# Two units' scores per visit to the 64-row products, masks added on VectorE, up-projections in groups of four

## The chip, the core and the metric

The kernel runs on one core of one Trainium2 chip, in one launch, in float32. Weights and activations of the large products are split into a high and a low part of a reduced format that the kernel calls fp32r; three products of the parts stand for one float32 product. The metric is the device time of one execution in microseconds; the kernel before takes 871.8 us (median of three runs, 871.6 to 871.97).

## The reference

The input x (256 tokens, 1024 wide) passes two blocks. The first: differential attention and stick-breaking attention side by side, cross attention on 256 memory tokens, and an MLP with squared ReLU. The second block is where most of the change lies: attention over compressed, selected and window keys (12 heads, called nsa below), and attention with dilations (12 heads in three groups of four, called dil), then gates, an output product and another MLP. In NumPy terms, cut to what matters:

```python
# first block, differential attention: two softmaxes per head, causal
p = softmax(where(causal, q k^T * scale, -inf)); w = p[0] - lam * p[1]; o = w v
# second block, dilated attention, g = 3 groups of 4 heads (window, dilation)
s = where((d >= 0) & (d % dil == 0) & (d <= win), q k^T * scale, -1e30)
o_g = softmax(s) v;  lse_g = log(sum(exp(s)));  y = sum_g softmax_over_g(lse)_g * o_g
# second block, nsa: for selected and window keys (at 256 tokens both are causal)
o_b = softmax(where(causal, q k^T * scale, -1e30)) v_b;   y += gate_b * o_b    # b = 1, 2
# MLP
h += square(relu(norm(h) @ w_up)) @ w_down          # w_up 1024 x 4096
```

## The kernel before, in words

Weights come in strips of 512 columns (or 512 rows) by SP's DMA queue into three buffers `raw`. ScalarE (ACT) copies each half strip to its high part (`hi`, L738), GpSimd (POOL) subtracts to the low part (L695), TensorE (PE) multiplies (`strip`, whose products are L1922 in three modes, and L1928 and L1929 in the mode `up`). The order of every engine's instructions is written out by hand; semaphores join them.

The mode `up` computes 128 output columns of an up-projection in one PSUM bank: for each of the 8 blocks of 128 input rows, `both` issues one product of 512 columns (high weights by x high and x low side by side) and one of 256 columns (low weights by x high). There are 16 such strips, with 32 pairs each.

Attention is cut into units (`units`). A unit has 512 score columns in two PSUM banks, one bank for heads in rows 0 to 63 of the array, one for heads in rows 64 to 127 (head width 64, so two score products run side by side in the halves of the array). Units 0 to 5 are the differential attention, 6 to 9 the cross attention, and from `U_A` on come 27 units of the second block: 9 dil (3 for the first 128 tokens with four heads each, 6 for the others with two heads and 256 keys), 6 nsa for the first 128 tokens (two heads, two branches), and 12 nsa for the others (two heads, one branch, 256 keys). `unit_loop` runs over the units with a lag, on each engine:

- PE, turn i: masks of unit i by an identity product of bfloat16 into both banks (L2079), the score products (L2086; each float32 product is two passes in the profile), then the `hook` (a share of a strip of the next projection, so that PE has work), then the transposes of the probabilities of unit i-1 (L2098), then the products with the values of unit i-2 (L2112) into bank 7.
- DVE (VectorE), turn i: row maximum of unit i (one TENSOR_REDUCE of 512 columns, L1358), the copy of the transposed probabilities of unit i-1 to SBUF (L1368), then `post` of unit i-2. `post_nsa` is a reciprocal (L1801), a product with the gates (L1803), a product of the values by these factors (L1805, after which PE may overwrite bank 7) and one addition to `xn` per branch (L1812). `post_dil` is a copy (L1817). For the differential units there is also `combine` (L1380 to L1388), on which the transposes wait.
- ACT: exponentials with a row sum (L787), after the maximum of the same unit.

The log-sum-exp over the dilations is one Ln and one Exp on ACT and some small operations on DVE (L1836 to L1849), after which POOL mixes the three groups (L675 to L681).

At the end of the second loop, turn `NU`, PE transposes two blocks of `xn` into banks 0 and 1 (`fill_block`, L2024), ACT and DVE split them (`fill_hi`, `fill_lo_block`, L1170), and the next strip (`IN2 + 13`), which writes banks 0 to 3, waits for these splits. DVE does the first of them (`fill_lo_block(0)`) in `post_nsa` of the last unit but one.

The line that decides the scores' banks before the change:

```python
half = bank(4 - (4 if n >= U_A else 2) * (n % 2), 2).rearrange("p (r x) -> p r x", r=2)[:, :, 0:256]
```

Of the kernel before, what the change touches and what calls it, by code (L numbers as in the profile page):

```python
# [20 lines left out]
S = 256  # L21
P = 128
NT = S // P
# [57 lines left out]
def build(nc, a, out):  # L81
# [3 lines left out]
    with ctx:  # L85
# [16 lines left out]
        mbf = sb("mbf", [P, P + C_ALL - C_SMALL], bf16)  # L102
# [3 lines left out]
        ST = sb("small", [P, 1702])  # L106
# [4 lines left out]
        def small(n):  # L111
            st_at[0] += n
            assert st_at[0] <= 1702, st_at[0]
            return ST[:, st_at[0] - n:st_at[0]]

# [8 lines left out]
        def maskb(col, n):  # L124
            return mbf[:, P + col - C_SMALL:P + col - C_SMALL + n]
# [72 lines left out]
        dl = [small(24) for _ in range(4)]  # L198
# [72 lines left out]
        dl_den, dl_ln, dl_arg, dl_exp = sem("dl_den"), sem("dl_ln"), sem("dl_arg"), sem("dl_exp")  # L271
# [265 lines left out]

        def scores_of(n):

            half = bank(4 - (4 if n >= U_A else 2) * (n % 2), 2).rearrange("p (r x) -> p r x", r=2)[:, :, 0:256]  # L540
            return half.rearrange("p r (s w) -> p r s w", w=units[n]["w"])
# [161 lines left out]
        def _(act):  # L703
# [69 lines left out]
            def exps(n):  # L773
# [3 lines left out]
                act.wait_ge(mx_done, n + 1)  # L777
# [287 lines left out]
            for n in range(U_A, NU):  # L1065
# [10 lines left out]
                if n == U_N + 4:  # L1076
# [19 lines left out]
        def _(dve):  # L1096
# [245 lines left out]
            V.tensor_copy(mbf[:, P:], msk).then_inc(masks_ready, 1)  # L1342
# [9 lines left out]
            def unit_loop(n0, n1, post, hook, early=lambda i: None):  # L1352
                for i in range(n0, n1 + 2):
                    if i < n1:
# [3 lines left out]
                        V.tensor_reduce(den_of(i)[1], scores_of(i), AX.X, ALU.max, negate=True).then_inc(mx_done, 1)  # L1358
# [10 lines left out]
                    if i - 2 >= n0:  # L1369
                        dve.wait_ge(pv_done, i - 1)  # L1370
                        post(i - 2, units[i - 2])
                    hook(i)
# [421 lines left out]
            def post_nsa(n, u):  # L1794

                if n == NU - 2:
                    fill_lo_block(0)
                k = len(u["segs"])
# [14 lines left out]

            def post_dil(n, u):
# [14 lines left out]
            lse = dl[1].rearrange("p (t g i) -> p t g i", t=NT, g=3)  # L1829
            d8v = [x.rearrange("p (t i) -> p t i", t=NT) for x in d8]  # L1830

            def dilation_lse():

                dve.wait_ge(post_done, U_N)
                signal(dl_den, 1)
                link(V.reciprocal(dl[2], dil_den))  # L1836

            def dilation_max():
                dve.wait_ge(dl_ln, 1)
                link(V.tensor_tensor(dl[1], dl[0], dil_nm, ALU.subtract))  # L1840
                link(V.tensor_reduce(d8v[0], lse.rearrange("p t g i -> p t i g"), AX.X, ALU.max))
                V.tensor_tensor(lse, lse, bc(d8v[0].unsqueeze(2), [P, NT, 3, 4]), ALU.subtract).then_inc(dl_arg, 1)

            def dilation_weights():
                dve.wait_ge(dl_exp, 1)
                link(V.tensor_reduce(d8v[1], lse.rearrange("p t g i -> p t i g"), AX.X, ALU.add))
                link(V.reciprocal(d8[2], d8[1]))
                link(V.tensor_tensor(dl[1], dl[1], dl[2], ALU.mult))
                link(V.tensor_tensor(lse, lse, bc(d8v[2].unsqueeze(2), [P, NT, 3, 4]), ALU.mult))  # L1849
            def hook2(i):  # L1850
                if i == U_N + 2:
                    dilation_lse()
                if i == U_N + 3:
# [656 lines left out]
```

## Time and profile before

| | |
|---|---|
| median of three runs | 871.8 us |
| the profiled execution's own time | 871.61 us |
| its span, first to last instruction | 869.7 us |
| granted TensorE clock over the span | 1.000 |
| PE busy | 861.6 us (99%) |
| DVE, ACT, POOL busy | 399.4, 457.0, 647.1 us |
| products of the mode `up` (L1928, L1929) | 512 of 512 columns, 512 of 256 columns |
| identity products that add masks (L2079) | 66 |

A matmul's duration in the profile holds its way through the array, so that consecutive products overlap: what one costs is the distance from its start to the next one's. Idle time of PE is shown only where no product is modelled as running.

### The profile page before, as it was taken

What the parts mean: (1) busy time and instruction counts of PE and PEld (TensorE: products, weight loads), DVE (VectorE), ACT (ScalarE), POOL (GpSimd) and SP (SyncE); (2) the same over time, 40 slices, a digit from 0 to 9 for tenths busy, and PEclk for the clock granted to TensorE, in tenths of its full rate; (3) what the DMA queues carried; (4) which work ended last, traced back from release to release, by engine and by line L of the source; (5) the groups of instructions that cost most, each with busy time, mean ns of one, the idle gap of its engine ahead of it and who ended that gap; (6) DMA issues with size and microseconds to landing.
All of it is one profiled execution on the core that took longest, in us unless ns stands there. A gap on an engine that the chain in (4) does not pass through costs nothing.

```text
span 869.7 us, 12258 instructions
## 1 busy us (share of the span) xinstructions
PE 861.6 (99%) x4846; PEld 724.8 (83%) x4846; DVE 399.4 (46%) x662; ACT 457.0 (53%) x622; POOL 647.1 (74%) x389
## 2 busy tenths in 40 slices
PE   9999999999999999999999999999999999999998
PEld 7898887898888888888887897777788888888886
DVE  5697652233321111113788699559965322111112
ACT  6674476356375444444763645636455475444440
POOL 3789473848679988888798889812638879888881
PEclk9999999999999999999999999999999999999999
DMA  9965252534546655555854554520233546755531
GB/s 332 337 226 195 96 194 97 171 121 138 176 123 220 239 193 193 193 185 157 288 166 131 187 177 137 160 92 1 98 98 130 163 165 223 239 193 187 184 112 48
DMA packets 65119, 147.09 MB, mean 169 GB/s; under 512 B 4880, under 2 KB 11056, under 8 KB 64944
## 3 DMA queue, kind: packets, MB, share of 16 engines
q1 hardware_dynamic: 65072, 146.45, 50.3%
q8 instruction: 31, 0.51, 0.2%
q14 instruction: 16, 0.13, 0.0%
HBM read 145.40 MB, written 1.05 MB: 168 GB/s over the span
## 4 chain that ended last, share of the span: by engine, by line
PE 87%; DVE 6%; POOL 2%; ACT 2%; DMA 2%; issue 1%; SPq 0%; ACTq 0%; DVEq 0%
PE ps L1922 54%; PE ps L1928 14%; PE ps L1929 7%; PE ps L2112 2%; POOL w_lo L695 2%; PE ps L2086 2%; PE ps L2024 1%; PE ps L2098 1%; DMA h<-in_x 1%; PE ps L2355 1%; DVE xn L1812 1%; DVE arena L1368 1%; DMA raw<-in_w_in 1%; PE ps L2273 1%; PE ps L2294 1%
## 5 line engine op out<-in xcount | busy, mean ns | idle before, releaser
L695 POOL TENSOR_TENSOR w_lo<-raw,w_hi 128x512 fp32r<-128x512 f32 (+2 forms) x364 | 636.2, 1788 | 168.9 <-ACT w_hi L738 168.9
L1922 PE MATMUL ps<-w_hi,x 128*128 128x512 f32 (+1 forms) x1344 | 431.1, 392 | 1.3 <-POOL w_lo L695 1.1
L738 ACT ACTIVATE w_hi<-raw 128x1024 fp32r<-128x1024 f32 (+3 forms) x193 | 247.7, 1320 | 171.2 <-PE ps L1922 54.1
L1922 PEld LDWEIGHTS ps<-w_hi,x 128*128 128x128 f32 x1344 | 251.3, 188 | 59.9 <-issue 6.5
L1922 PE MATMUL ps<-w_lo,x 128*128 128x512 f32 (+1 forms) x672 | 259.6, 386 | 0.0
L1928 PE MATMUL ps<-x,w_hi 128*128 128x512 f32 x512 | 181.5, 398 | 0.0
L1922 PEld LDWEIGHTS ps<-w_lo,x 128*128 128x128 f32 x672 | 126.4, 188 | 22.5
L1929 PE MATMUL ps<-x,w_lo 128*128 128x256 f32 x512 | 143.5, 280 | 0.0
L1928 PEld LDWEIGHTS ps<-x,w_hi 128*128 128x128 f32 x512 | 96.2, 188 | 23.9 <-DVE x L1532 0.5
L1525 DVE TENSOR_TENSOR ps<-ps,arena 128x1024 f32<-128x1024 f32 x16 | 19.7, 1233 | 198.4 <-ACT arena L942 198.4
L1929 PEld LDWEIGHTS ps<-x,w_lo 128*128 128x128 f32 x512 | 96.7, 189 | 0.4
L1922 PE MATMUL ps<-x,w_hi 128*128 128x256 f32 x384 | 71.5, 287 | 0.0
L1922 PEld LDWEIGHTS ps<-x,w_hi 128*128 128x128 f32 x384 | 59.9, 191 | 1.9 <-issue 1.4
L787 ACT ACTIVATE arena<-ps,small 128x128 f32<-128x128 f32 (+1 forms) x80 | 32.9, 420 | 52.0 <-DVE small L1358 52.0
L1922 PE MATMUL ps<-x,w_lo 128*128 128x256 f32 x192 | 54.3, 283 | 0.0
L756 ACT ACTIVATE x<-ps 128x512 fp32r<-128x512 f32 x24 | 14.2, 595 | 50.2 <-DVE ps L1165 37.3
L942 ACT ACTIVATE arena<-ps 128x1024 f32<-128x1024 f32 x16 | 16.4, 1022 | 40.9 <-PE ps L1929 40.9
L1922 PEld LDWEIGHTS ps<-x,w_lo 128*128 128x128 f32 x192 | 36.6, 191 | 0.0
L1528 DVE TENSOR_TENSOR ps<-ps,arena 128x1024 f32<-128x1024 f32 x16 | 19.7, 1232 | 28.6 <-ACT arena L947 28.6
L2112 PE MATMUL ps<-arena 128*128 128x64 f32 (+1 forms) x240 | 31.1, 270 | 0.8 <-DVE gain L1805 0.7
L2112 PEld LDWEIGHTS ps<-arena 128*128 128x128 f32 x240 | 29.4, 192 | 1.6 <-issue 1.4
L675 POOL TENSOR_TENSOR arena<-arena,small 128x768 f32<-128x768 f32 x2 | 3.0, 1502 | 35.7 <-DVE small L1112 35.7
(284 smaller groups left out, 815.6 us busy)
## 6 DMA issues: line engine op xcount, KB each, us to landing
raw<-in_w_up SPq DMA_DIRECT2D x32, 1024.0 KB, 5.3
raw<-in_w_down SPq DMA_DIRECT2D x32, 1024.0 KB, 4.9
raw<-in_w_in SPq DMA_DIRECT2D x31, 1024.0 KB, 5.3
raw<-in_w_xkv SPq DMA_DIRECT2D x8, 1024.0 KB, 5.0
raw<-in_w_out SPq DMA_DIRECT2D x8, 1024.0 KB, 4.9
raw<-in_w_xq SPq DMA_DIRECT2D x4, 1024.0 KB, 5.0
raw<-in_w_xo SPq DMA_DIRECT2D x4, 1024.0 KB, 4.9
raw<-in_w_in SPq DMA_DIRECT2D x6, 512.0 KB, 8.5
```

The lines of the kernel that those rows point to most:

```text
L695: x = nc.gpsimd.tensor_tensor(LO[s % 2][:, 2048 * q + d0:2048 * q + d1], RAW[n % 3][:, d0:d1], HI[s % 2][:, 2048 * q + d0:2048 * q + d1].b ...
L738: nc.scalar.activation(HI[s % 2][:, 2048 * q + c0:2048 * q + c1], RAW[n % 3][:, c0:c1], ACT.Copy).then_inc(hi_done, 1)
L756: nc.scalar.activation(dst[:, :, P * t:P * t + P], src, ACT.Copy).then_inc(tb_hi, 1)
L787: x = nc.scalar.activation(dst, sc[:, i // per, i % per, :], ACT.Exp, bias=nm[:, i // per, i % per:i % per + 1], accum_out=dn[:, i // per, ...
L942: nc.scalar.activation(up_rows(act_c), up_out(j, 1), ACT.Copy).then_inc(up_taken, 1)
L1525: V.tensor_tensor(up_out(j), up_out(j), up_rows(act_c), ALU.add).then_inc(up_sum, 1)
L1528: V.tensor_tensor(up_out(j), up_out(j), up_rows(act_c), ALU.mult).then_inc(sq_ready, 1)
L1922: last = T.matmul(dst, l, r, start=start and i == 0, stop=stop and i == 2, skip_group_check=w_stationary)
L1928: T.matmul(dst, wh, hl, start=start, stop=stop, skip_group_check=True)
L1929: return T.matmul(dst[:, 0:S], wl, hl[:, 0:S], start=False, stop=stop, skip_group_check=True)
L2086: last = T.matmul(sc[:, r, k, :], q, kk, start=first, stop=x == len(qk) - 1, skip_group_check=True)
L2112: last = T.matmul(values_of(n)[:, sg["vw"] * si:sg["vw"] * si + sg["vw"]], pt[:, c:c + P], sg["v"][k], start=k == 0, stop=k == nk - 1)
```

## The change

1. Units of kinds diff, dil and nsa (without the nsa units of the first 128 tokens, and the cross units) have `own_mask`: PE adds no mask. DVE replaces the one TENSOR_REDUCE by `maxima`: for each of the unit's score tiles one TENSOR_TENSOR_REDUCE that reads the tile from PSUM and the mask (bfloat16, SBUF), writes -(score + mask) back to PSUM, and gives the row minimum of that. ACT's exponential then has scale -1. (Two of them per unit of 256 keys, four per unit of 128 keys.)
2. In the second loop the scores go by `GROUPS`: the first unit alone, then twelve pairs, then the last two units one by one. `group_scores` computes both units of a pair in one visit, each in 256 columns of the same two banks; pairs alternate between banks 4, 5 and 0, 1. Transposes now run at turn i for unit i-2 and the value products for unit i-3, so that the loop has one turn more (30 instead of 29).
3. nsa units with one branch: `coefs_nsa` (reciprocal and two TENSOR_SCALAR of one column) runs before the wait for the values, and `post_single` adds each head's 64 columns from PSUM to `xn` by one SCALAR_TENSOR_TENSOR, instead of L1803, L1805 and L1812.
4. No logarithm: the weights over the dilations are exp(m - max m) times the row sums, normalised; the Ln and five small DVE operations go, two come.
5. In the mode `up`, `group_of_four` issues four products of 512 columns, then the four of 256 columns, instead of pairs.
6. The first four steps of strip `IN2 + 13` move from behind the loop to the hook of turn 29, ahead of the last unit's value products; PE waits at turn 27 for the exponentials of unit NU-2 ahead of `fill_block`.

```diff
@@ units and banks
+            if u["kind"] in ("diff", "nsa"):
+                u["own_mask"] = mbf[:, 3 * P - u["w"]:3 * P]
+            if u["kind"] == "dil":
+                u["own_mask"] = u["mask"][1]
+            if u["kind"] == "nsa" and u["t"] == 0 or u["kind"] == "cross":
+                u["own_mask"] = None
+        GROUPS = [(U_A,)] + [(n, n + 1) for n in range(U_A + 1, NU - 2, 2)] + [(NU - 2,), (NU - 1,)]
@@ ACT, exps
-                act.wait_ge(mx_done, n + 1)
+                act.wait_ge(mx_done, (GROUPS[group_of[n]][-1] if n >= U_A else n) + 1)
+                                             scale=1.0 if u["own_mask"] is None else -1.0,
@@ ACT, behind the exponentials of unit n
-                if n == U_N + 2:
-                    act.wait_ge(dl_den, 1)
-                    nc.scalar.activation(dl[0], dil_den, ACT.Ln).then_inc(dl_ln, 1)
@@ DVE
+            def maxima(n, u):
+                sc, nm, per = scores_of(n), den_of(n)[1], len(u["segs"]) // 2
+                if u["own_mask"] is None:
+                    V.tensor_reduce(nm, sc, AX.X, ALU.max, negate=True).then_inc(mx_done, 1)
+                    return
+                for r in range(2):
+                    for k in range(per):
+                        x = V.tensor_tensor_reduce(sc[:, r, k, :], sc[:, r, k, :], u["own_mask"], -1.0, 3.0e38,
+                                                   ALU.add, ALU.min, nm[:, r, k:k + 1])
+                x.then_inc(mx_done, 1)
+            def group_loop(post, hook, early, before):
+                for i in range(U_A, NU + 3):
+                    if i < NU and GROUPS[group_of[i]][0] == i:
+                        ns = GROUPS[group_of[i]]
+                        dve.wait_ge(sc_done, ns[-1] + 1)
+                        for n in ns:
+                            maxima(n, units[n])
+                    early(i)
+                    if U_A <= i - 2 < NU:
+                        n = i - 2
+                        u = units[n]
+                        dve.wait_ge(tr_done, n + 1)
+                        dve.wait_ge(pv_done, n - 1)
+                        c = slice(0, P * u["blocks"])
+                        V.tensor_copy(u["pr"][2 + n % 2][:, c], bank(6)[:, c]).then_inc(pt_done, 1)
+                    if i - 3 >= U_A:
+                        before(i - 3, units[i - 3])
+                        dve.wait_ge(pv_done, i - 2)
+                        post(i - 3, units[i - 3])
+                    hook(i)
+            def post_single(n, u):
+                if n == NU - 2:
+                    fill_lo_block(0)
+                for m in range(2):
+                    c = 64 * (u["hs"][0] + m)
+                    y = xn[:, u["t"], c:c + 64]
+                    last = V.scalar_tensor_tensor(y, values_of(n)[:, 64 * m:64 * m + 64], coef[:, m:m + 1], y,
+                                                  ALU.mult, ALU.add)
+                last.then_inc(post_done, 1)
+                dve.wait_ge(post_done, n + 1)
@@ PE
-            def both(dst, hl, wh, wl, start, stop):
-                T.matmul(dst, wh, hl, start=start, stop=stop, skip_group_check=True)
-                return T.matmul(dst[:, 0:S], wl, hl[:, 0:S], start=False, stop=stop, skip_group_check=True)
+            def group_of_four(dst, hl, wh, wl, c, w, k0):
+                for q in range(4):
+                    T.matmul(dst, wh[:, c + w * q:c + w * q + P], hl[:, 512 * (k0 + q):512 * (k0 + q) + 512],
+                             start=k0 + q == 0, stop=k0 + q == KT - 1, skip_group_check=True)
+                for q in range(4):
+                    last = T.matmul(dst[:, 0:S], wl[:, c + w * q:c + w * q + P],
+                                    hl[:, 512 * (k0 + q):512 * (k0 + q) + S],
+                                    start=False, stop=k0 + q == KT - 1, skip_group_check=True)
+                return last
+            def group_loop(hook):
+                for i in range(U_A, NU + 3):
+                    if i < NU and GROUPS[group_of[i]][0] == i:
+                        group_scores(group_of[i])      # masks of units without own_mask, then all scores
+                    hook(i)
+                    if U_A <= i - 2 < NU:              # waits ex_done(n + 1), pt_done(n); transposes of n = i - 2
+                        ...
+                    if i - 3 >= U_A:                   # waits pt_done(n + 1), post_done(n); values of n = i - 3
+                        ...
                 elif k == 27:
+                    pe.wait_ge(ex_done, NU - 1)
                     fill_block(0)
                     fill_block(1)
-            unit_loop(U_A, NU, hook2)
-            strip(IN2 + 13, 0, 4, {0: tb[0] - 1, 2: tb[0]})
+                elif k == 29:
+                    strip(IN2 + 13, 0, 4, {0: tb[0] - 1, 2: tb[0]})
+            group_loop(hook2)
```

## Rows read from the trace of the kernel before

**Rows 1.** The page, part 1: busy time of each engine.
```profile
PE 861.6 (99%) x4846; PEld 724.8 (83%) x4846; DVE 399.4 (46%) x662; ACT 457.0 (53%) x622; POOL 647.1 (74%) x389
```

**Rows 2.** A stretch: us; busy PE, PEld, DVE, ACT, POOL; clock; DMA share, GB/s.
```profile
595.00:634.00 39.00, 37.63 (x264) 28.38 (x264) 35.84 (x86) 19.74 (x66) 20.90 (x18) 1.00 0.16 55
```

**Rows 3.** Timeline of PE around the first dil unit: start, us, instructions.
```profile
551.70 0.39 PE L1922 MATMUL ps<-w_lo,x 128*128 128x512 f32 x1
...
552.15 0.39 PE L2079 MATMUL ps<-mbf 128*128 128x256 bf16 x2
552.48 0.71 PE L2086 MATMUL ps<-arena 64*128 64x128 f32 x8
553.12 0.50 PE L1922 MATMUL ps<-w_hi,x 128*128 128x512 f32 x1
553.46 0.39 PE L1922 MATMUL ps<-w_lo,x 128*128 128x512 f32 x1
```

**Rows 4.** Timeline of PE around a one-branch nsa unit.
```profile
631.88 0.60 PE L2098 MATMUL ps<-cst,arena 128*128 128x128 f32 x4
632.31 1.00 PE L2112 MATMUL ps<-arena 128*128 128x64 f32 x8
633.15 0.28 PE L2079 MATMUL ps<-mbf 128*128 128x128 bf16 x2
633.36 0.70 PE L2086 MATMUL ps<-arena 64*128 64x256 f32 x4
633.99 0.50 PE L1922 MATMUL ps<-w_hi,x 128*128 128x512 f32 x1
```

**Rows 5.** Timeline of PE: a strip that follows value products, no scores between.
```profile
640.01 0.47 PE L1922 MATMUL ps<-w_hi,x 128*128 128x512 f32 x1
640.33 0.40 PE L1922 MATMUL ps<-w_lo,x 128*128 128x512 f32 x1
```

**Rows 6.** Timeline of PE in an up strip, eight pairs apart.
```profile
381.04 0.40 PE L1928 MATMUL ps<-x,w_hi 128*128 128x512 f32 x1
...
383.87 0.40 PE L1928 MATMUL ps<-x,w_hi 128*128 128x512 f32 x1
```

**Rows 7.** Timeline of PE in a strip of 256-column products, 24 products apart.
```profile
80.23 0.28 PE L1922 MATMUL ps<-x,w_lo 128*128 128x256 f32 x1
...
83.11 0.28 PE L1922 MATMUL ps<-x,w_lo 128*128 128x256 f32 x1
```

**Rows 8.** Timeline of PE: a place of the second loop where it is late.
```profile
619.56 0.65 PE L2098 MATMUL ps<-cst,arena 128*128 128x128 f32 x4
620.57 1.07 PE L2112 MATMUL ps<-arena 128*128 128x64 f32 x8 [0.36 <-DVE gain L1805]
```

**Rows 9.** Timeline of DVE in the second loop.
```profile
614.62 0.68 DVE L1368 COPY arena<-ps 128x512 f32<-128x512 f32 x1
615.22 0.15 DVE L1801 RECIPROCAL small<-small 128x2 f32<-128x2 f32 x1
615.40 0.96 DVE L1803 TENSOR_TENSOR small<-small 128x2 f32<-128x2 f32 x1
...
622.18 0.16 DVE L1803 TENSOR_TENSOR small<-small 128x2 f32<-128x2 f32 x1
```

**Rows 10.** Timeline of POOL in the second loop.
```profile
610.03 10.05 POOL L695 TENSOR_TENSOR w_lo<-raw,w_hi 128x512 fp32r<-128x512 f32 x8
```

**Rows 11.** Timeline of DVE in the first loop, differential units.
```profile
95.45 0.61 DVE L1403 SCALAR_TENSOR_TENSOR arena<-ps,small,xn 128x128 f32<-128x128 f32 x2
96.09 0.69 DVE L1358 TENSOR_REDUCE small<-ps 128x2 f32<-128x512 f32 x1
...
97.20 0.48 DVE L1388 SCALAR_TENSOR_TENSOR arena<-ps,small,arena 128x256 f32<-128x256 f32 x1
```

**Rows 12.** Timeline of PE in the first loop: transposes that wait for DVE.
```profile
97.74 0.44 PE L2098 MATMUL ps<-cst,arena 128*128 128x128 f32 x2 [0.79 <-DVE arena L1388]
```

**Rows 13.** Timeline of ACT at the start of the second loop.
```profile
557.12 2.01 ACT L738 ACTIVATE w_hi<-raw 128x1024 fp32r<-128x1024 f32 x2
```

More of the change, by code:

```diff
@@ L197, in build @@
         cden = small(24)
-        dl = [small(24) for _ in range(4)]
+        dl = [small(24) for _ in range(2)]
         d8 = [small(8) for _ in range(3)]
@@ L536, in values_of @@
             return bank(4 if n == NU - 1 else 7)
+        GROUPS = [(U_A,)] + [(n, n + 1) for n in range(U_A + 1, NU - 2, 2)] + [(NU - 2,), (NU - 1,)]
+        group_of = {n: m for m, ns in enumerate(GROUPS) for n in ns}
         def scores_of(n):
-            half = bank(4 - (4 if n >= U_A else 2) * (n % 2), 2).rearrange("p (r x) -> p r x", r=2)[:, :, 0:256]
+            if n >= U_A:
+                m = group_of[n]
+                b, c = 4 - 4 * (m % 2), 256 * GROUPS[m].index(n)
+            else:
+                b, c = 4 - 2 * (n % 2), 0
+            half = bank(b, 2).rearrange("p (r x) -> p r x", r=2)[:, :, c:c + 256]
             return half.rearrange("p r (s w) -> p r s w", w=units[n]["w"])
@@ L1350, in _, with unit_loop @@
             evac(5, u_vs, rows=rstd_n[:, 0:2])
-            def unit_loop(n0, n1, post, hook, early=lambda i: None):
+            def maxima(n, u):
[8 more added lines that the diff above has]
+                x.then_inc(mx_done, 1)
+            def unit_loop(n0, n1, post, hook, early=lambda i: None, before=lambda n, u: None):
                 for i in range(n0, n1 + 2):
@@ L1792, in _, with coefs_nsa, post_double @@
                 tb_take(lambda src: V.tensor_copy(kbT[:, 512 * b:512 * b + 512], src))
-            def post_nsa(n, u):
+            def coefs_nsa(n, u):
+                if u["kind"] != "nsa" or len(u["branches"]) == 2:
+                    return
+                h0, g = u["hs"][0], 1 + u["branches"][0]
+                link(V.reciprocal(coef[:, 0:2].rearrange("p (r s) -> p r s", r=2), den_of(n)[0]))
+                for m in range(2):
+                    c = coef[:, m:m + 1]
+                    V.tensor_scalar(c, c, g4[:, u["t"], h0 + m, g:g + 1], None, ALU.mult).then_inc(dve_step, 1)
+                chain[0] += 2
+                dve.wait_ge(dve_step, chain[0])
+            def post_single(n, u):
                 if n == NU - 2:
                     fill_lo_block(0)
+                for m in range(2):
+                    c = 64 * (u["hs"][0] + m)
[4 more added lines that the diff above has]
+                dve.wait_ge(post_done, n + 1)
+            def post_double(n, u):
                 k = len(u["segs"])
@@ L2113, in unit_loop, with group_scores @@
                                                 pt[:, c:c + P], sg["v"][k], start=k == 0, stop=k == nk - 1)
+                        last.then_inc(pv_done, 1)
+            def group_scores(m):
+                ns = GROUPS[m]
+                if m >= 2:
+                    pe.wait_ge(ex_done, GROUPS[m - 2][-1] + 1)
+                begun = [False, False]
+                for n in ns:
+                    u, sc = units[n], scores_of(n)
+                    if u["own_mask"] is not None:
+                        continue
+                    c, mk = u["mask"]
+                    for r in range(2):
+                        T.matmul(sc[:, r, :, c:c + mk.shape[1]], identb,
+                                 mk.unsqueeze(1).broadcast_to([P, len(u["segs"]) // 2, mk.shape[1]]),
+                                 start=not begun[r], stop=False, skip_group_check=True)
+                        begun[r] = True
+                for n in ns:
+                    u, sc = units[n], scores_of(n)
+                    per = len(u["segs"]) // 2
+                    for k in range(per):
+                        for r in range(2):
+                            q, kk = u["segs"][per * r + k]["qk"][0]
+                            last = T.matmul(sc[:, r, k, :], q, kk, start=not begun[r], stop=True, skip_group_check=True)
+                            begun[r] = True
+                last.then_inc(sc_done, len(ns))
@@ new lines, in group_loop @@
+            def group_loop(hook):
[4 more added lines that the diff above has]
+                    if U_A <= i - 2 < NU:
+                        n = i - 2
+                        u = units[n]
+                        pe.wait_ge(ex_done, n + 1)
+                        pe.wait_ge(pt_done, n)
+                        for q in range(u["blocks"]):
+                            last = T.transpose(bank(6)[:, P * q:P * q + P], u["pr"][n % 2][:, P * q:P * q + P], ident)
+                        last.then_inc(tr_done, 1)
+                    if i - 3 >= U_A:
+                        n = i - 3
+                        u = units[n]
+                        pe.wait_ge(pt_done, n + 1)
+                        if n < NU - 1:
+                            pe.wait_ge(post_done, n)
+                        pt = u["pr"][2 + n % 2]
+                        nk = u["w"] // P
+                        for si, sg in enumerate(u["pv"]):
+                            for k in range(nk):
+                                c = u["w"] * si + P * k
+                                last = T.matmul(values_of(n)[:, 64 * si:64 * si + 64], pt[:, c:c + P], sg["v"][k],
+                                                start=k == 0, stop=k == nk - 1)
```

57 lines of the change are left out of this document (29 added, 28 removed).

## The prediction

> **What bounds the kernel.** I read the busy times first: PE is busy 861.6 of 869.7 us, no other engine above 74% [rows 1]. So a gain is what PE issues less, a loss is what makes PE wait. The profiled execution took 871.61 us, 1.9 more than its span and 0.2 less than the median; the sum is a difference against 871.6, and I set it on the median, 871.8. The second view is busy time by stretch: in the nsa part of the second loop PE idles 1.37 of 39 us, DVE is busy 35.8 of 39, and the granted clock is 1.00, the 2.4 GHz level [rows 2]. There DVE is the engine that can make PE late. The third is PE's timeline, where I take distances from start to start.
>
> **The bubble of a visit to the 64-row products.** A 512-column product costs 0.225 (two from 551.70 to 552.15 [rows 3]), so two masks of 256 columns should cost 0.11 each, but the scores start 0.33 behind the first: 0.10 is lost on entry. The scores then hold PE 0.64. A plain float32 pass of 128 columns costs 0.43 / 4 = 0.108 (the transposes [rows 4]), four of them 0.43: 0.21 lost. The strip's first product takes 0.34 in place of 0.23: 0.11 lost. Sum 0.41 us a visit, to 0.01 or 0.02. With 256 keys it is alike [rows 4]: 0.21 behind two masks of 0.056, and 0.63 for two passes of 0.215.
>
> **1. Visits merged (gain 3.8).** 27 visits become 15. A skipped visit does not save all: the strip then follows value products, and its first product takes 0.32 anyway [rows 5], so 0.09 stays. 12 x (0.41 - 0.09) = 3.8 us. Bounds: 0, if every unit of a pair exposes its own weight load and drain, and 4.9 if all 0.41 goes. I take 3.8: the heads inside the visit of rows 3 already run without a bubble between them.
>
> **2. Masks off PE (gain 3.3).** Removed in the second loop: 18 products of 256 columns at 0.11 (9 dil units) and 24 of 128 columns at 0.056 (12 nsa units) [rows 3, 4]: 2.0 + 1.3 = 3.3 us. The entry bubble stays. The last value product takes 0.105 although it has 64 columns (0.84 for eight [rows 4]), so the step from it to the scores may shrink too, by at most 0.08 in some nine visits, 0.7; I take none. In the first loop 4 wide and 8 narrow masks go, 0.9 us; see step 5.
>
> **3. The price on DVE.** No row shows a TENSOR_TENSOR_REDUCE. The nearest is SCALAR_TENSOR_TENSOR, which also reads PSUM and one SBUF tensor: 0.48 for 256 columns, and two of 128 columns within 0.61 [rows 11]; less the 0.08 by which a copy's end overlaps its successor [rows 9] that is 0.40 and 0.27 from start to start. From below: the plain reduction of 512 columns, as long as the copy, 0.60 from start to start. From above: each followed by a second instruction as long as a two-column one, 0.16 [rows 9]. So T, the price of a unit of 256 keys, was 0.60 and is 0.60 to 1.15; I take 0.85, near the two SCALAR_TENSOR_TENSOR. For 128 keys four of them, 1.1.
>
> What goes on DVE: L1803, L1805 and L1812 for 12 units, against two one-column operations ahead of the wait and two SCALAR_TENSOR_TENSOR of 64 columns (0.2 each, by the slope of rows 11). A second effect weighs more: L1803, two columns wide, takes 0.96 at 615.40 and 0.16 at 622.18 [rows 9]. Both its operands lie in SBUF; the long case falls in the 10 us in which POOL runs without a pause, the short one behind them [rows 10]. The new operations read at most one SBUF tensor, as L1368 at 614.62 does none and is not held. So DVE gets steadier.
>
> **4. Waits of PE in the second loop (net gain 0.8).** Late now: from the transposes at 619.56 to the values it takes 1.01 [rows 8] where 0.43 is normal [rows 4]. With the like at 596, 608 to 610 and 616 I add up 2.5 us beyond the normal distances. They follow held operations, or the log-sum-exp chain ahead of a maximum; the lag grows by a turn of nearly 3 us, which covers them. Gain 2.5; bounds 1.0 and 2.5.
>
> Added waits, each with what queues behind it:
> - Pairs. From the end of a value product PE does scores 0.10 + 0.32 + 3 x 0.215 + 0.10 = 1.17, two strip shares of 0.78 (16 shares in 14 turns, each three products of 0.225, and the 0.09), two sets of transposes of 0.43 and one of values of 0.90: 4.5 us until the next values, which need bank 7 read. Meanwhile DVE waits for the scores 1.17 and a signal 0.1, then has 2T, copy 0.6, factors 0.35, two additions 0.45 queued in front of that signal: 2.67 + 2T. It is late from T = 0.92. At 0.85 nothing, at 1.15 0.5 for each of six pairs. I take 0.2, bounds 0 and 3. Dil pairs have only a copy there, and are late from T = 1.1.
> - Start. Pair (1, 2) makes DVE reduce eight tiles, 2.2 us, before ACT may begin with unit 1. ACT then has four exponentials (1.4), the high part of a half strip (2.0 [rows 13]) and four more queued; PE reaches the transposes of unit 2 about 1 us before these end. I take 0.9, bounds 0.2 and 2.
> - End. Turn 28 has no strip share, and turn 29's needs banks 0 and 1 free. After the value products of unit NU-2 DVE runs fill_lo_block(0), as long as a copy, 0.68 and a signal, and nothing of PE lies between, where it had the last value products (0.9): 0.8. PE waits some 0.3 in this place now, which goes, and the two early transposes ahead of it may wait 0.1 for bank 7: 0.6, bounds 0.2 and 1.5.
> - The Ln and the small operations are off PE's path; they count in the 2.5 alone. The memset comes where DVE idles.
>
> 2.5 - 0.2 - 0.9 - 0.6 = 0.8.
>
> **5. First loop (0).** At 97.74 PE has waited 0.79 for combine [rows 12]. The DVE chain of copy, post, maximum and combine behind it [rows 11] starts at the end of strip 6. Masks removed before that (0.55 us) are a gain; from there DVE sets the next two sets of transposes, T in place of 0.60 costs 0.25 twice, and the 0.3 of later masks only lengthens PE's wait: 0.55 - 0.5, nothing. Bounds: loss 0.8, gain 0.6.
>
> **6. Up-projections in fours (gain 2.4).** A pair costs 2.83 / 8 = 0.354 [rows 6]. Runs of one length are at 0.225 to 0.227 for 512 columns [rows 3] and 2.88 / 24 = 0.120 for 256 [rows 7]. Four and four cost three distances of each and one pair: 0.681 + 0.360 + 0.354 = 1.395, against 4 x 0.354 = 1.415: 0.02, by 128 groups 2.6 us; 2.4 for the rounding of the rows. Bounds: 0 (the distance in a run of the short ones is no less than in the pair, 0.354 - 0.227 = 0.127) and 4.
>
> **Sum.** 3.8 + 3.3 + 0.8 + 0 + 2.4 = 10.3, less 0.9 that I keep back for ACT and POOL, from which the strips behind the loop now ask their parts earlier: 9.4. 871.8 - 9.4 = 862.4 us.
>
> **Rivals.**
> - A. The up order is worth nothing: 864.8. For it: every 512-column product needs the same time for its columns, every load of 128 columns of weights too, and the order changes neither number. Against it: the distances of rows 3 and 7. The Trainium skill ("TensorE: Matmul & The Clock Gate", section "Back-to-back issue gap") has N/2.4 + 2.5 ns for N columns, by which both orders cost the same; its 0.325 for a pair does not agree with the trace's 0.354.
> - B. Merging saves no bubble, each unit pays its own: 862.4 + 3.8 = 866.2. Against it the heads of rows 3.
> - C. DVE and ACT are late, with a second instruction behind each reduction: T = 1.15, pairs late by 0.5 (2.8 more than taken), start 2 (1.1 more), first loop 0.6 more: 862.4 + 4.5 = 866.9. The Trainium skill ("VectorE: DVE Perf Modes", section "Two Vector instructions with no wait between them") states that an operation which writes out its accumulator is two instructions. No DVE row here shows one.
> - D. More gain: bubbles whole (1.1), entry shorter (0.7), up at 4 (1.6), start at 0.2 (0.7): 862.4 - 4.1 = 858.3.
> - E. Slower. The instruction costs twice a SCALAR_TENSOR_TENSOR of its width, T = 1.7, and DVE sets the pace: six nsa pairs late by 1.6, three dil pairs by 1.2, start 3, first loop 3, end 0.6, in all 19.8 of waits, against 3.8 + 3.3 + 2.4 + 2.5 + 0.6 = 12.6: 879.0 us. It decides from about T = 1.4. For it: DVE is at 92% there [rows 2], and no row has the instruction. Against it: one pass over the same columns.
>
> **Chances.** Forecast 0.57, A 0.12, B 0.05, C 0.11, D 0.10, E 0.05. The range 857.5 to 867.5 holds the forecast and most of A to D. A measurement tells a difference of about 0.2% (1.7 us) from none. Faster by more than that: all but E and a tail of C, 0.93; within it 0.03; slower 0.04.
>
> **What would show it.** 12 rows of L2079, not 66; L2086 of a pair at distances of 0.215 behind the first; the long up products at 0.227 and the short ones at 0.120 inside their runs; PE idle under 1 us from 595 on; the new operation near 0.48 for 256 columns; no SBUF operation of the post near 1 us; a wait of 0.8 ahead of strip IN2+13. Wrong would be: T over 1.0 with a wait of L2112 in each pair, a bubble between the units of a pair, or an unchanged distance in the up strips.

## The result and the profile after

The changed kernel takes 873.4 us (median of 20 runs, 872.2 to 875.0) against 871.8 of the kernel before; the ratio is 1.0017, 95% interval 1.0010 to 1.0023. I had forecast 862.4. It is 1.6 us slower where 9.4 were to be gained. One execution can differ from the next by a fall of TensorE's granted clock in the second loop, worth 1 to 2.5 us; where a difference below is of that size, I compare executions whose clock stayed at 1.00.

What was to be bought is there: a visit for two units answers to [rows 3, 4]. Eight score products in one row of 1.14, the strip 1.07 behind their start, 0.33 for its first product (PE's timeline: start, us, instructions):

```profile
617.65 1.14 PE L2216 MATMUL ps<-arena 64*128 64x256 f32 x8
618.72 0.50 PE L1993 MATMUL ps<-w_hi,x 128*128 128x512 f32 x1
619.05 0.39 PE L1993 MATMUL ps<-w_lo,x 128*128 128x512 f32 x1
```

The page, part 1, answers to [rows 1]:

```profile
PE 857.6 (98%) x4792; PEld 725.5 (83%) x4792; DVE 403.5 (46%) x773; ACT 453.8 (52%) x619; POOL 647.2 (74%) x389
```

PE is busy 4.0 us less, though part of it ran at half clock, and yet the span grew from 869.7 to 871.9: idle time. The stretches say where (columns as in [rows 2], whose stretch is the first line):

```profile
595.00:634.00 39.00, 33.73 (x208) 26.54 (x208) 33.74 (x116) 14.69 (x47) 20.87 (x18) 0.91 0.17 55
```

PE idles 5.3 of the 39 us, not 1.4, and the clock is 0.91, not 1.00. The same view, in finer stretches around the falls:

```profile
603.00:606.70 3.70, 1.14 (x8) 0.68 (x6) 3.63 (x12) 1.02 (x4) 3.70 (x4) 1.00 0.01 2
606.80:613.50 6.70, 5.58 (x22) 4.13 (x21) 6.09 (x17) 1.02 (x4) 4.51 (x4) 0.50 0.65 183
613.60:640.80 27.20, 25.72 (x182) 21.54 (x181) 21.58 (x90) 13.97 (x39) 5.95 (x5) 1.00 0.19 70
640.90:644.20 3.30, 3.30 (x9) 2.53 (x8) 0.95 (x4) 0.00 (x0) 3.30 (x4) 0.50 0.02 5
```

(The lines are successive stretches of one execution.) Twice the clock is at its lower level, 1.2 GHz: for 6.8 us behind a stretch in which PE was busy 1.14 of 3.70 us, and for 3.4 us behind a wait at 639. In the kernel before it never leaves 2.4 GHz in this loop.

PE's timeline there (in brackets the idle time ahead and who ended it):

```profile
603.37 0.40 PE L1993 MATMUL ps<-w_hi,x 128*128 128x512 f32 x1
606.33 0.72 PE L2232 MATMUL ps<-cst,arena 128*128 128x128 f32 x4 [2.56 <-DVE arena L1415]
608.17 1.94 PE L2245 MATMUL ps<-arena 128*128 128x64 f32 x8 [1.11 <-DVE gain L1875]
610.04 2.08 PE L2216 MATMUL ps<-arena 64*128 64x256 f32 x8
...
640.40 0.47 PE L1993 MATMUL ps<-w_hi,x 128*128 128x512 f32 x1 [0.93 <-DVE x L1182]
```

Transposes wait 2.56 for DVE's copy, values 1.11 for DVE's post. The second scores of line 610.04 show the halved clock: 2.08 us for what takes 1.14 at 617.65. The last line is the wait for `fill_lo_block(0)`.

DVE's timeline: the additions of one post at 591, then the posts of two units with two branches at 600 to 608:

```profile
591.22 0.62 DVE L1882 TENSOR_TENSOR xn<-xn,gain 128x128 f32<-128x128 f32 x2
...
600.69 0.65 DVE L1873 TENSOR_TENSOR small<-small 128x4 f32<-128x4 f32 x1
601.37 0.42 DVE L1875 TENSOR_TENSOR gain<-ps,small 128x256 f32<-128x256 f32 x1
601.83 2.15 DVE L1882 TENSOR_TENSOR xn<-xn,gain 128x128 f32<-128x128 f32 x2
604.00 0.43 DVE L1373 CUSTOM_DVE_ANT_0 ps<-ps,mbf 128x256 f32<-128x256 f32 x1
604.36 0.14 DVE L1373 DVE_READ_ACCUMULATOR2_ANT small<- 128x1 f32 x1
604.36 0.47 DVE L1373 CUSTOM_DVE_ANT_0 ps<-ps,mbf 128x256 f32<-128x256 f32 x1
...
605.50 0.69 DVE L1415 COPY arena<-ps 128x512 f32<-128x512 f32 x1
606.10 0.17 DVE L1871 RECIPROCAL small<-small 128x4 f32<-128x4 f32 x1
606.31 1.25 DVE L1873 TENSOR_TENSOR small<-small 128x4 f32<-128x4 f32 x1
```

The two additions to `xn` (L1882, L1812 before) take 2.15 us here and 0.62 at 591.22. L1875, which reads PSUM, keeps its 0.42. POOL's timeline answers to [rows 10]:

```profile
595.12 1.48 POOL L689 TENSOR_TENSOR arena<-arena,small 128x768 f32<-128x768 f32 x1 [26.06 <-DVE small L1124]
...
601.27 10.04 POOL L709 TENSOR_TENSOR w_lo<-raw,w_hi 128x512 fp32r<-128x512 f32 x8
```

Its unbroken run now begins at 595.12 with the mixing and at 601.27 with the low parts. In the kernel before, the mixing began at 603.90 and the low parts at 610.03 [rows 10], and one post with two branches, the last, lay under the run; its two additions took 1.24:

```profile
603.90 1.48 POOL L675 TENSOR_TENSOR arena<-arena,small 128x768 f32<-128x768 f32 x1 [35.70 <-DVE small L1112]
```

```profile
605.89 1.24 DVE L1812 TENSOR_TENSOR xn<-xn,gain 128x128 f32<-128x128 f32 x2
```

Now the run falls on the posts of the last three such units. Theory H: POOL holds their operations with two SBUF tensors, the next maxima and the copy come late, ACT and PE wait for them, and PE's idling brings the clock down. The Trainium skill ("SBUF — State Buffer", section "SBUF: two separate sides") states the hold as an exclusive lock for a whole instruction, between a VectorE operation with two SBUF inputs and a GpSimd operation that reads SBUF; the rows agree (L1873 held to 1.25 us, a POOL instruction of the low part being 10.04 / 8 = 1.26).

### The profile page after: what moved, and what is told of

Read it like the earlier page. It is cut to its first block, busy times and chain, and to the rows that moved or that the text cites. A ratio compares the mean times of both kernels' runs of the same rounds, so it can differ in the third digit from the quotient of the medians.

```text
span 871.9 us, 12260 instructions
## 1 busy us (share of the span) xinstructions
PE 857.6 (98%) x4792; PEld 725.5 (83%) x4792; DVE 403.5 (46%) x773; ACT 453.8 (52%) x619; POOL 647.2 (74%) x389
## 4 chain that ended last, share of the span: by engine, by line
PE 81%; DVE 8%; ACT 3%; DMA 3%; POOL 3%; issue 2%; SPq 0%; DVEq 0%; ACTq 0%
PE ps L1993 52%; PE ps L2000 12%; PE ps L2003 6%; POOL w_lo L709 3%; PE ps L2245 2%; DMA raw<-in_w_in 2%; PE ps L2216 1%; PE ps L2101 1%; ACT w_hi L752 1%; PE ps L2232 1%; DMA h<-in_x 1%; DVE xn L1882 1%; DMA raw<-in_w_up 1%; DVE ps L1373 1%; PE ps L2406 1%
## 5 line engine op out<-in xcount | busy, mean ns | idle before, releaser
L1993 PE MATMUL ps<-w_hi,x 128*128 128x512 f32 (+1 forms) x1344 | 431.7, 393 | 2.1 <-POOL w_lo L709 1.0
L1993 PEld LDWEIGHTS ps<-w_hi,x 128*128 128x128 f32 x1344 | 252.5, 189 | 57.1 <-issue 5.2
L1993 PE MATMUL ps<-w_lo,x 128*128 128x512 f32 (+1 forms) x672 | 260.6, 388 | 0.0
L1993 PEld LDWEIGHTS ps<-w_lo,x 128*128 128x128 f32 x672 | 127.0, 189 | 22.8
L2000 PE MATMUL ps<-x,w_hi 128*128 128x512 f32 x512 | 140.0, 395 | 0.2 <-DVE x L1580 0.2
L2000 PEld LDWEIGHTS ps<-x,w_hi 128*128 128x128 f32 x512 | 88.2, 189 | 13.3 <-DVE x L1580 1.1
L2003 PEld LDWEIGHTS ps<-x,w_lo 128*128 128x128 f32 x512 | 78.5, 189 | 10.9
L2003 PE MATMUL ps<-x,w_lo 128*128 128x256 f32 x512 | 81.4, 281 | 0.0
L1993 PE MATMUL ps<-x,w_hi 128*128 128x256 f32 x384 | 71.5, 287 | 0.1
L1993 PEld LDWEIGHTS ps<-x,w_hi 128*128 128x128 f32 x384 | 59.9, 191 | 2.0 <-issue 1.5
L1993 PE MATMUL ps<-x,w_lo 128*128 128x256 f32 x192 | 54.3, 283 | 0.0
L1993 PEld LDWEIGHTS ps<-x,w_lo 128*128 128x128 f32 x192 | 36.7, 191 | 0.0
L2245 PE MATMUL ps<-arena 128*128 128x64 f32 x216 | 28.5, 276 | 2.2 <-DVE gain L1875 1.6
L2245 PEld LDWEIGHTS ps<-arena 128*128 128x128 f32 x216 | 27.1, 197 | 3.9 <-issue 3.8
L1580 DVE TENSOR_TENSOR x<-ps,x 128x1024 fp32r<-128x1024 f32 x16 | 19.6, 1225 | 19.0 <-ACT x L969 19.0
```

Of the source, the lines that this page charges most:

```text
L1580: V.tensor_tensor(up_rows(XL[abuf][:, c]), up_out(j), up_rows(XH[abuf][:, c].bitcast(f32)), ALU.subtract).then_inc(a_lo, 1)
L1993: last = T.matmul(dst, l, r, start=start and i == 0, stop=stop and i == 2, skip_group_check=w_stationary)
L2000: T.matmul(dst, wh[:, c + w * q:c + w * q + P], hl[:, 512 * (k0 + q):512 * (k0 + q) + 512], start=k0 + q == 0, stop=k0 + q == KT - 1, skip ...
L2003: last = T.matmul(dst[:, 0:S], wl[:, c + w * q:c + w * q + P], hl[:, 512 * (k0 + q):512 * (k0 + q) + S], start=False, stop=k0 + q == KT - ...
L2245: last = T.matmul(values_of(n)[:, 64 * si:64 * si + 64], pt[:, c:c + P], sg["v"][k], start=k == 0, stop=k == nk - 1)
```

## Experiments

**e1: POOL released later.** POOL's mixing waits for the signal `dl_weights`. U_N is the first nsa unit; at turn U_N + 8 DVE has done the post of the last unit with two branches.

```diff
-                if i == U_N + 5:
+                if i == U_N + 8:
                     dilation_weights()
                     signal(dl_weights, 1)
```

> The changed kernel with one line moved: the weights over the dilations are made, and POOL is released, at turn U_N + 8 in place of U_N + 5, behind the last double-branch unit's post. Theory H (POOL holds the two-SBUF-operand additions of the double-branch posts, PE waits about 6 us at 596 to 608 and its clock then falls for 6.8 us, worth 3.4): the operations of L1873 and L1882 stay under 0.35 us each, PE's lateness at 596 to 608 falls from 6 to about 1 us, no fall of the clock near 607, and the time is 873.4 - 5 - 3.4 = about 865. Rival R1 (the new maximum's instruction makes DVE late): unchanged, since no such instruction goes, 873. Rival R2 (the lag of three turns and the grouping are late by themselves): 872 to 873.

Measured: 864.8 us (864.4 to 865.8), ratio 0.9922 [0.9905, 0.9938]. DVE's groups of the second loop, in the changed kernel and then in e1 (busy us, mean ns):

```profile
L1882 DVE TENSOR_TENSOR xn<-xn,gain 128x128 f32<-128x128 f32 x12 | 7.8, 654 | 0.4
L1873 DVE TENSOR_TENSOR small<-small 128x4 f32<-128x4 f32 x6 | 2.6, 428 | 0.2
```

```profile
L1882 DVE TENSOR_TENSOR xn<-xn,gain 128x128 f32<-128x128 f32 x12 | 3.5, 292 | 0.4
L1873 DVE TENSOR_TENSOR small<-small 128x4 f32<-128x4 f32 x6 | 1.0, 165 | 0.2
```

5.9 us of holds are gone from DVE, and the stretch reads:

```profile
595.00:634.00 39.00, 36.99 (x253) 30.08 (x252) 33.55 (x137) 19.75 (x56) 22.50 (x20) 1.00 0.24 83
```

POOL runs from 604.17 on, beside posts that read one SBUF tensor; their pairs of SCALAR_TENSOR_TENSOR stay at 0.48. 8.5 us come back, as theory H has it. The new maximum (R1) and the lag with the groups (R2) are all still there, so neither is the cause. The small operations of the weights moved as well; e5 parts them from POOL.

**e5: the small operations early, POOL late.** Only `signal(dl_weights, 1)` moves to turn U_N + 8.

> The changed kernel with the four small operations of dilation_weights where they were (turn U_N + 5), but the signal that releases POOL only at turn U_N + 8. It parts the two sides of e1. Theory H: the small operations ahead of the maximum cost the 1.0 us of lateness at 596 at most, POOL's run the rest, so 865 to 866. Rival (the small operations in front of pair (15, 16)'s maximum start the whole chain of waits, POOL only lengthens it): 870 or more.

Measured: 865.9 us, ratio 0.9927 [0.9912, 0.9942]. Its transposes at 597.60 still wait 0.80 behind the small operations, and nothing long follows:

```profile
597.60 0.63 PE L2233 MATMUL ps<-cst,arena 128*128 128x128 f32 x4 [0.80 <-DVE arena L1415]
```

With the clock at 1.00 it takes 865.0 and 865.3, e1 864.4 to 864.9. So POOL's run is the cause, and the chain of the weights some 0.4 us of the 8.5 (1.0 by the medians).

**e2: the hold avoided on DVE's side.** POOL early as in the changed kernel, but the double posts without an operation on two SBUF tensors.

```diff
-                link(V.tensor_tensor(cv, cv, g4[:, t, h0:h0 + 2, 1 + b0:1 + b0 + nb], ALU.mult))
...
-                for b in range(nb):
-                    link(V.tensor_tensor(y, y, wv[:, :, b], ALU.add))
+                        V.tensor_scalar(c, c, g4[:, t, h0 + m, 1 + b:2 + b], None, ALU.mult)     # m, b in 0, 1
...
+                        x = V.scalar_tensor_tensor(y, values_of(n)[:, q:q + 64], coef[:, 2 * m + b:2 * m + b + 1], y,
+                                                   ALU.mult, ALU.add)
+                x.then_inc(post_done, 1)
```

> The changed kernel with the double-branch posts as in the single ones: four factors by TENSOR_SCALAR and four SCALAR_TENSOR_TENSOR of 64 columns that read PSUM, no operation with two SBUF tensors; POOL starts where it does in the changed kernel. Theory H: the post takes about 1.5 us also beside POOL, PE is late only by the 1.05 at 596 (the chain of the dilation weights ahead of the maximum stays) and some tenths, the clock does not fall near 607: 873.4 - 4.5 - 3.4 = about 865.5. Rival R1 or R2: 873, or more, since DVE issues four instructions more for each of six units.

Measured: 870.8 us (869.2 to 872.4), ratio 0.9988 [0.9978, 0.9998]. With the clock at 1.00 it is 869.2 and 869.8, still 4.7 above e1. Half right: the operations are not held beside POOL (0.99 for four, as at 591.57, ahead of its run):

```profile
598.91 0.58 DVE L1874 TENSOR_SCALAR small<-small 128x1 f32<-128x1 f32 x4
599.52 0.99 DVE L1881 SCALAR_TENSOR_TENSOR xn<-ps,small,xn 128x64 f32<-128x64 f32 x4
600.54 0.69 DVE L1415 COPY arena<-ps 128x512 f32<-128x512 f32 x1
```

But I forgot what else the post does: L1875 emptied bank 7 0.42 us into it, and the additions came behind that signal. Now they stand ahead of it, and PE's values wait:

```profile
598.94 0.63 PE L2239 MATMUL ps<-cst,arena 128*128 128x128 f32 x4 [1.18 <-DVE arena L1415]
600.66 1.08 PE L2252 MATMUL ps<-arena 128*128 128x64 f32 x8 [1.09 <-DVE xn L1881]
```

Three such waits of 1.1 us, which end at 592.70, 600.66 and 607.67, and the wait for this copy, 1.18, stand in the place of those of the changed kernel: PE's idle time in the second loop is 6.6 us, against 7.0 there and 2.4 in e1. What is gained is mostly the clock. So e2 shows that the hold goes with the two SBUF tensors; that nothing else of POOL's early run costs time it does not show, for a kernel without holds and with the old signal was not tried.

**e4: PE kept busy through the waits.** 20 and 8 products of a zero tensor are added to bank 2 in turn 18, ahead of the two long waits; nothing else changes.

```diff
+                        if i == U_A + 18:
+                            add_zeros(20)      # T.matmul(bank(2)[:, 0:256], identb, zeros, start=False, stop=False)
                         pe.wait_ge(ex_done, n + 1)
```

> The changed kernel with 28 products of zeros (256 columns, bfloat16, added to bank 2) put ahead of the two longest waits of PE, 20 ahead of the transposes and 8 ahead of the values of turn 18 (about 2.1 and 0.9 us, inside the idle 2.56 and 1.11 us). If the fall of the clock at 607 follows PE's idling: the waits' ends stay, the clock does not fall, 873.4 - 3.4 = about 870. If the clock falls for another reason (heat, total work, or zeros count as idle): 873.4 or a little more.

Measured: 870.6 us (870.3 to 872.1), ratio 0.9988 [0.9978, 0.9998].

```profile
603.73 2.36 PE L2223 MATMUL ps<-mbf 128*128 128x256 bf16 x20
606.45 0.63 PE L2240 MATMUL ps<-cst,arena 128*128 128x128 f32 x4 [0.37 <-DVE arena L1415]
606.91 1.04 PE L2223 MATMUL ps<-mbf 128*128 128x256 bf16 x8
608.30 1.08 PE L2255 MATMUL ps<-arena 128*128 128x64 f32 x8 [0.35 <-DVE gain L1875]
609.30 1.13 PE L2216 MATMUL ps<-arena 64*128 64x256 f32 x8
```

The waits end where they did (606.45 and 608.30, against 606.33 and 608.17), and yet 2.8 us are gained: in the profiled execution the clock stays at 1.00 to the end of the loop. So of the 8.5 us of e1 the lower clock is 2.8 and the waits, by subtraction, 5.7, and the first fall came from PE's idling.

**e3 and e6: the first steps of strip IN2+13 behind the loop again**, in the changed kernel (e3) and with e1 (e6).

```diff
-                elif k == 29:
-                    strip(IN2 + 13, 0, 4, {0: tb[0] - 1, 2: tb[0]})
             group_loop(hook2)
+            strip(IN2 + 13, 0, 4, {0: tb[0] - 1, 2: tb[0]})
```

> The changed kernel with the first four steps of strip IN2+13 behind the loop again, after the last value products. Theory H: the value products (0.9 us) cover the wait for fill_lo_block(0); the 1.1 us of lateness at 639 falls to 0.3, the clock does not fall at 641 (worth 1.7): 873.4 - 2.5 = about 871. If the second fall of the clock comes from something else, 872.6. The stalls at 596 to 608 and the first fall stay.

> e1 and e3 together: POOL released at turn U_N + 8 and the first steps of strip IN2+13 behind the loop. In e1 the wait of 1.12 ahead of that strip stayed and no fall of the clock followed it, so the 0.9 of value products that cover it are all that is to gain: 864.8 - 0.9 = 863.9. If the two interact by the clock again: 862.

Measured: e3 871.7 us, ratio 0.9997 [0.9987, 1.0007], 1.7 less than the changed kernel; e6 863.9 us (863.7 to 864.0), ratio 0.9908 [0.9893, 0.9923], 0.9 less than e1. The last 16 value products run through and the strip follows without the 0.93:

```profile
639.30 1.97 PE L2245 MATMUL ps<-arena 128*128 128x64 f32 x16 [0.33 <-DVE xn L1861]
641.31 0.47 PE L1993 MATMUL ps<-w_hi,x 128*128 128x512 f32 x1
```

In e3's profile the fall at 641 is gone, but the one behind 605 lasts 10.2 us in place of 6.8, so the profile does not part clock and cover in the 1.7. The list of executions does in part: at a mean clock of 0.994 e3 takes 872.4 (median of 4) against 873.6 (18), at 0.996 871.3 (6) against 872.3 (2). So about 1.1 is left at an equal clock, and some 0.6 is clock. In e6 0.9 is the value products' cover. The moved steps do a second thing: the wait ahead of the strip brings the clock down in some executions only. In e5's profiled one it did (stretches of its trace, the wait of 0.93 in the first):

```profile
630.00:634.00 4.00, 2.65 (x20) 2.23 (x20) 3.71 (x13) 3.16 (x4) 0.76 (x1) 1.00 0.22 91
634.30:637.50 3.20, 3.20 (x9) 2.46 (x8) 0.94 (x4) 0.00 (x0) 3.20 (x4) 0.50 0.02 5
```

e5's four executions are 865.0 and 865.3 us at a clock of 1.00 and 866.5 and 867.1 at 0.998; all four of e6 lie within 0.3 us at 1.00. Over the kernels with the late release, 9 of 20 executions with the strip in turn 29 (e1, e5, e8, e9, e10) have a mean clock of 0.998, and none of the 8 with the strip behind the loop (e6, e11) is below 0.999.

**e7: the up-projections in fours alone**, in the kernel before.

> The kernel before with the up-projections in groups of four and nothing else. My step said -2.4. The changed kernel's trace has 0.234 between the long products of a group, not 0.227, so by it 512 pairs take 178.2 in place of 178.9 us: -0.7, 871.2. Rival A (worth nothing): 871.9.

Measured: 870.5 us (870.1 to 871.1), ratio 0.9985 [0.9975, 0.9994]: 1.4 us, interval 0.5 to 2.2. The timeline of the changed kernel answers to [rows 6]:

```profile
381.60 1.09 PE L2000 MATMUL ps<-x,w_hi 128*128 128x512 f32 x4
382.53 0.63 PE L2003 MATMUL ps<-x,w_lo 128*128 128x256 f32 x4
383.00 1.09 PE L2000 MATMUL ps<-x,w_hi 128*128 128x512 f32 x4
```

A group takes 383.00 - 381.60 = 1.40 us, between the 1.395 of my step and the 1.415 of four pairs. Summed over all 512 pairs (without the step out of each strip), the distances fall from 178.9 to 178.0 us: 0.9. Inside a group the long ones stand at 0.234, the short ones at 0.118; in the pairs of the kernel before it was 0.236 and 0.117.

**e8 and e12: the masks of the second loop back on PE**, with e1 (e8) and with POOL's early release (e12).

```diff
-            if u["kind"] == "nsa" and u["t"] == 0 or u["kind"] == "cross":
+            if u["kind"] == "nsa" and u["t"] == 0 or u["kind"] == "cross" or u["kind"] in ("dil", "nsa"):
                 u["own_mask"] = None
```

> e1 with the masks of the second loop back on PE (identity products, plain TENSOR_REDUCE), groups and all else as in e1. My step 2 priced the masks at 3.3 us, and DVE's dearer maximum at 0 to 0.4: 864.8 + 3.3 = 868.1. If the dearer maximum takes most of it back, 865 to 866. If DVE paced the loop by it (rival C or E), 863.

> The changed kernel (POOL released at turn U_N + 5 as in it) with the masks of the second loop back on PE: what e8 is to e1. It asks whether the new maximum's instruction has a part in the long waits at 596 to 608. With the early release POOL's run is the cause and the maximum only adds its own 0.4 us a pair: 873.4 + 1.8, less at most 1 for two maxima that come between held operations = 874 to 875. If the dearer maximum is what makes DVE late there (rival R1), the waits and the fall of the clock go and it is 867 to 869.

Measured: e8 866.7 us, ratio 0.9944 [0.9929, 0.9959]; with the clock at 1.00 865.8 against e1's 864.8. e12 874.8 us, ratio 1.0032 [1.0020, 1.0043], 1.4 more than the changed kernel. In e12 two plain maxima stand between the held additions and the copy, and PE waits nearly as long:

```profile
603.31 2.15 DVE L1882 TENSOR_TENSOR xn<-xn,gain 128x128 f32<-128x128 f32 x2
605.49 1.29 DVE L1369 TENSOR_REDUCE small<-ps 128x2 f32<-128x512 f32 x2
606.70 0.68 DVE L1415 COPY arena<-ps 128x512 f32<-128x512 f32 x1
```

```profile
607.53 0.63 PE L2232 MATMUL ps<-cst,arena 128*128 128x128 f32 x4 [2.27 <-DVE arena L1415]
```

The new instruction is no cause of the loss. Masks on DVE are worth 1.0 us net by the times of e8, 1.3 by the spans of the profiled executions (863.8 and 862.5). Waits that only appear with them take back 1.9: PE's waits ahead of the values in each pair and the one at the start, which I sum as distances beyond the usual one, are 3.8 us in e1 and 1.9 in e8. So the masks themselves are worth 2.9 to 3.2.

**e10: no pairs.** e1 with `GROUPS = [(n,) for n in range(U_A, NU)]`.

> e1 with every unit a group of its own: the lag of three turns, the masks on DVE and all else stay, the 12 merged visits are undone. My step 1 priced them at 3.8; the waits of 0.24 to 0.28 (and 0.43) ahead of the second values of a pair, 1.5 us in all, and the 0.48 at the start should go with the pairs: 864.8 + 3.8 - 2.0 = 866.6. Rival B (no bubble is saved by merging): 862.8.

Measured: 867.1 us, ratio 0.9958 [0.9941, 0.9975]; at a clock of 1.00 866.2, 1.45 more than e1. Its waits sum to 2.05, 1.8 less than e1's, so that the merging by itself saves 1.45 + 1.8 = 3.2 (3.7 by the spans of the profiled executions, 864.4 and 862.5). Rival B falls. The waits of the pairs need both parts of the change: six of them, 1.7 us, in e1, one of 0.26 without the new maximum (e8), none without pairs (e10).

**e9: the first loop's masks on PE**, else e1.

> e1 with the masks of the six differential units of the first loop back on PE, with plain TENSOR_REDUCE. My step 5 priced this part at 0 (bounds -0.8 and +0.6): 864.8. In e1's trace the products behind that loop start 0.67 us earlier than in the kernel before (111.94 against 112.61), so if that is the masks' doing, 865.5.

Measured: 865.5 us, ratio 0.9929 [0.9913, 0.9946]; at a clock of 1.00 864.65 and 864.86, as e1. The transposes of [rows 12] wait 0.79 in e9 and 0.92 with the masks on DVE:

```profile
97.16 0.44 PE L2176 MATMUL ps<-cst,arena 128*128 128x128 f32 x2 [0.92 <-DVE arena L1436]
```

The 0.67 that I read from one pair of traces is in part scatter: up to this point the changed kernel and ten of my variants are the same program, and the scores behind the loop start between 111.93 and 112.63 in them (mean 112.2). The kernel before and e7, the same up to here, have 112.60 and 112.69, and e9 has 112.43. So the change gains some 0.4 to 0.5 up to there, on the average. Whether the masks are a part of it stays open: e9's one trace would give them 0.3, which is within the scatter, and its times show nothing.

**e11: the factors ahead of the scores.** In e6, `before(i - 3, ...)` moves from behind the copy to the beginning of DVE's turn.

> e6 with the factors of the single-branch units (reciprocal and two TENSOR_SCALAR, 0.55 us) computed at the beginning of the turn, ahead of the wait for the scores, where DVE idles 0.2 to 0.6 us. They no longer stand between the copy and the additions that free bank 7: the waits at 608, 614 and 620 (0.43, 0.23, 0.23) go, 863.9 - 0.9 = 863.0. If DVE's total and not the order sets these waits, 863.9.

Measured: 863.0 us (862.9 to 863.4), ratio 0.9904 [0.9887, 0.9921]: 8.6 us less than the kernel before beside it (871.6), 10.4 less than the changed one. In the last two nsa pairs the values follow the transposes without a wait:

```profile
613.98 0.60 PE L2233 MATMUL ps<-cst,arena 128*128 128x128 f32 x4
614.42 1.00 PE L2246 MATMUL ps<-arena 128*128 128x64 f32 x8
```

At 608 the wait has only moved. The factors now stand ahead of the maxima, and the copy behind these, which frees the transposes' bank, starts at 607.86 in place of 607.24 (e6). PE idles ahead of the transposes:

```profile
608.69 0.63 PE L2233 MATMUL ps<-cst,arena 128*128 128x128 f32 x4 [0.30 <-DVE arena L1417]
```

By distances, 0.47 of the gain comes from the pairs at 614 and 620, none from 608, and 0.28 from the value products at the end, which wait 0.13 and not 0.33. I had expected 0.43 from 608 and nothing from the end: the forecast of 863.0 was met by luck in part.

## Why the prediction was wrong, step by step

**The step that failed is the second effect of step 3, "So DVE gets steadier".** I had seen the hold, named its condition (two SBUF tensors, POOL running) and looked at the new operations only. The double-branch posts keep three such operations each. I never asked where POOL's run would fall: its release is one turn earlier, the posts are one turn later, so that three double posts lie under it where one did. DVE's holds on them (5.9 us more than in e1) are what the runs showed in place of a steadier DVE. They cost 8.5 us (e1, e5), of which 2.8 is a price that had no term at all, the clock (e4). It made slower what rivals A to D all called faster, and my one slower rival, E, put the reason into T.

**T was a little less than taken.** A custom instruction of 256 columns takes 0.43 to 0.47 us and its accumulator read begins 0.35 behind its start; the next starts with the read, so a unit of 256 keys costs 2 x 0.38 = 0.76. I took 0.85. Rivals C and E fall by it. The rule cited under C, that such an operation is two instructions ("VectorE: DVE Perf Modes", the Trainium skill), is borne out by the rows of DVE_READ_ACCUMULATOR2_ANT, 0.14 us each, but most of it lies beside the main ones.

**Steps 1 and 2** (3.8 and 3.3): 3.2 to 3.7 by e10, 2.9 to 3.2 by e8.

**Step 4.** The 2.5 us of lateness went (e1). The pairs cost 1.7, not 0.2: T was less than taken, but two TENSOR_SCALAR with the reciprocal take 0.55, not 0.35, the scores' signal came 1.4, not 1.27, after the last values, and all of this stands in front of the signal that frees bank 7. e11 shows that it is the order at 614 and 620: with the factors moved ahead the two waits there go. The largest, at 608, does not, it moves to the transposes. The start costs 0.5, not 0.9. The end costs 1.45 in place of 0.6: the 0.93 idle, a distance of 1.1 beyond the usual one, was foreseen as 0.8; a second wait, 0.33 ahead of the last but one value products (0.5 as a distance), was taken as 0.1; and the 0.3 taken as going was 0.16.

**Step 5** (0): 0 by e9's times, with some tenths left open by the traces; inside the bounds.

**Step 6** (2.4): 0.9 by the distances, 1.4 by e7's median. I took the distance in a run of long products from rows of another strip mode, 0.227; in a run of four behind short ones it is 0.234, hardly less than the 0.236 of a pair.

**The 0.9 kept back** for ACT and POOL did not come. From the first product of strip IN2+13 to the end it takes 229.7 us in the kernel before and in e1 alike. e1 has value products of 0.84 more there, and less by the order of the up products (half of step 6's 0.9) and by 0.24 in the strip's first steps, which leaves nothing for a wait.

With e1's release the sum would have been off by 2.4 us, inside the range: 864.8. Part of that is luck: the 0.9 that did not come hides a part of what steps 4 and 6 were off. For the kernel as it is, the range was too narrow by one mechanism.

## What to carry to other kernels

When a change shifts one engine's work by a turn, lay the unbroken runs of the others beside it again: an operation that can be held is dear or cheap by what runs beside it, and an untouched line can become the costliest. Where PE is the bound, a stall costs more than its length if the clock falls behind it (here 2.8 us beside 5.7 of waits). Moving one signal by three turns was worth 8.5 us, more than the two main edits of the change. And before an operation is replaced by a faster form, ask which signal the old form gave in its middle: in e2 the answer cost three waits of 1.1 us.

## What the runs showed of the hardware that I had not expected

- A wait of 0.93 us, with 0.33 some 2 us ahead of it, is followed by a granted clock of 0.50, the 1.2 GHz level, for 3.4 us in some executions of one kernel and not in others (e5's profiled one and e1's); without it there was no such fall (e6, e11). Products of zeros, put into the waits of 2.56 and 1.11 us, kept it at 1.00 (e4).
- The reduction that also writes its masked input costs 0.38 us for 256 columns from start to start, with most of the accumulator read (0.14) beside the next one (e1, 611.27 to 612.77).
- Products of 512 columns stand at 0.227 in the strips of L1993 and at 0.234 inside the groups of four of the mode `up` (the changed kernel); which weights or banks make the difference was not tried.
